# Keys, values and queries by Strassen's scheme: seven half-size products for eight in five of six column groups

## The chip, the cores and the metric

One core of one Trainium2 chip runs the whole program. The metric is the device time of one execution in microseconds (us); lower is better. The core has five engines that run side by side and meet at semaphores: TensorE (PE, matmuls; PEld is its weight load), VectorE (DVE), ScalarE (ACT), GpSimd (POOL) and SyncE (SP, which here only issues DMAs). PE writes PSUM, which has eight banks of 512 f32 columns on 128 partitions; POOL can't read PSUM.

## The reference, cut to what matters

One inference step of a two-layer decoder trunk, for 1024 prompt tokens and 64 sample tokens (1088 rows), D = 1024, all in float32. Layer 0 is a recurrent layer, layer 1 is differential attention over keys and values projected from the normed residual. The change touches only this:

```python
k, v = jnp.split(rms_norm(h, g) @ w_kv, [W_DIFF], axis=-1)            # W_DIFF = 768
k = rope(rms_norm(k.reshape(bsz, t, DIFF_HEADS, 2, DIFF_HD), k_g), pos)   # heads of 64
q, mem_q, gate = jnp.split(xn @ w_in, [W_DIFF, W_DIFF + W_MEM], axis=-1)
q = rope(rms_norm(q.reshape(bsz, t, DIFF_HEADS, 2, DIFF_HD), q_g), pos)
```

So three products of a 1088 x 1024 matrix with a 1024 x 768 one; keys and queries are then normed by head and rotated, and keys and values are also outputs.

## The kernel before

The program is a row of stages, each closed by a barrier. The stage that is changed, `keys_values_queries` (tiles named kvq_...), stands between `last_sums_and_norm` (which leaves the normed residual transposed in `xT`, and already computes tiles 2 and 3 of the first group, AHEAD) and the memory attention of layer 1.

The 2304 output columns are cut into six groups of W = 384 columns: k0, v0, k1, v1, q0, q1 (`GRP`). The rows are cut into NTILE = 9 tiles: NT = 8 prompt tiles of 128 rows and one sample tile of 64. For group i PE runs, for each prompt tile, KC = 8 matmuls (one for each 128 rows of the contraction) of `xT` 128 x 128 against 384 columns of `w[i % 2]` into one of the PSUM banks 0 to 5 (L2165), and for the sample tile 16 small ones (L2162). A float32 matmul shows in the trace as two instructions, so a tile of 384 columns is 16. The buffer `w` is double: SP loads the weights of group i when the products of group i - 2 are done (L2097), and POOL multiplies them by the norm's gain (`gained_weights`, L2111) before PE may start on them.

ACT takes each tile out of PSUM: for v a copy to `V`; for k and q a square (L2223) and a copy to `raw` (L2224). DVE reduces the squares by head (L2260). When the nine tiles of a group are there, ACT turns the sums into inverse roots (L2227, L2228, each with a table load), and DVE norms and rotates the whole group in eight operations over all nine tiles (L2263 to L2274) into `rot`, while PE is in the next group. Then PE transposes `rot` tile by tile through banks 6 and 7 (`turn`, L2147), and ACT copies to `KT` or `QT` (`turn_out`, L2188). POOL also issues the stores of k from `rot` (L2127) and of v from `V` (L2122).

At the end of the stage come the memory queries and gates (class `MemoryQueries`, `mem`): six jobs m on PE of 1088 columns each, with their weights loaded by SP (`mem.load`) and multiplied by the gain on POOL (L1422), and the weights of the first gates (`gates.load_ahead`, `gates.pool_ahead`, L1592). PE's order behind the last group is: turns of q0, jobs 0 and 1, turns of q1, jobs 2 to 5. `mem.act` of jobs 0 and 1 squares what `mem.dve` copied out of PSUM (L1472), and it stands ahead of the turns of q1 on ACT; on DVE `mem.dve` stands behind the norm of q1.

An instruction wrapped in `link(...)` is waited for by its own engine before the next is issued.

## Time and profile before

| | |
|---|---|
| median of 3 runs | 2091.23 us (2090.42 to 2688.17) |
| the profiled execution, its own time | 2090.91 us |
| its span in the profile | 2088.9 us |
| PE busy | 1937.7 us, 93% of the span |
| DVE, ACT, POOL busy | 42%, 30%, 17% |
| the stage's products, first to last group | 1152.4 to 1417.7 us |

A profile is one execution. Each instruction has a start and a duration; "idle before" is how long its engine stood still in front of it, with the instruction (engine, tile, line) that released it. PE's clock has two levels here, 2.4 GHz (shown as 1.00) and 1.2 GHz (0.50).

### The profile page before, as it was taken

Reading aid. Unit: us, or ns where it says so; the run is one execution under the profiler, and the core shown is the slowest. Engines: PE = TensorE matmul, PEld = TensorE weight load, DVE = VectorE, ACT = ScalarE, POOL = GpSimd, SP = SyncE. Lnnn points to the kernel's source line nnn. Section 1 sums busy time; section 2 is a strip of 40 time slices with the busy share of each in tenths; the row PEclk is TensorE's granted clock in tenths of the full one; section 3 lists DMA queues with packets and bytes.
Section 4 is the critical chain, followed back from the end, with each engine's and each line's share of the span. In section 5 each row is a group of like instructions: output and inputs, shape, how many; then the busy total and the mean of one; then the engine's idle time right before and its main releaser. Section 6 shows DMA issues by size and latency. Waiting matters only on the chain. (4 is left out here: it accounts for less than half of the span.)

```text
span 2088.9 us, 43622 instructions
## 1 busy us (share of the span) xinstructions
PE 1937.7 (93%) x19054; PEld 1251.2 (60%) x19054; DVE 882.9 (42%) x1785; ACT 616.7 (30%) x1447; POOL 346.6 (17%) x295
## 2 busy tenths in 40 slices
PE   6999989999999899997998999998999899799997
PEld 3576575675756757654444555555556566566664
DVE  4354372552734536323324324054123688733232
ACT  6322222222222222122214212222233466611111
POOL 0100030120300303020001130321000466311010
PEclk9999999999999999999999999999999999899998
DMA  8010010100100101008002120300110100566662
GB/s 285 18 36 13 11 34 26 32 20 21 34 22 17 39 21 33 23 17 314 1 31 86 61 95 31 134 11 10 41 61 21 61 1 1 203 223 223 216 221 76
DMA packets 53936, 147.61 MB, mean 71 GB/s; under 512 B 11587, under 2 KB 21123, under 8 KB 52468
## 3 DMA queue, kind: packets, MB, share of 16 engines
q1 hardware_dynamic: 43764, 103.97, 14.6%
q0 software_dynamic: 9984, 40.87, 5.6%
q8 instruction: 150, 2.46, 0.5%
q14 instruction: 38, 0.31, 0.0%
HBM read 123.58 MB, written 21.24 MB: 69 GB/s over the span
## 5 line engine op out<-in xcount | busy, mean ns | idle before, releaser
L772 PE MATMUL psum<-xT,rw_w 128*128 128x384 f32 (+1 forms) x1152 | 403.3, 489 | 0.0
L772 PEld LDWEIGHTS psum<-xT,rw_w 128*128 128x128 f32 x1152 | 206.4, 191 | 115.9 <-issue 11.3
L2165 PE MATMUL psum<-kvq_w,xT 128*128 128x384 f32 x384 | 124.6, 487 | 0.0
L1362 DVE SCALAR_TENSOR_TENSOR rwkv_xs<-psum,rwkv_pc,rwkv_xsc 128x64 f32<-128x64 f32 x90 | 25.5, 284 | 230.0 <-PE psum L1027 230.0
L2165 PE MATMUL psum<-spare,xT 128*128 128x384 f32 x352 | 114.3, 487 | 1.5 <-PEq L169 1.5
L740 POOL DMA_DIRECT2D out<-rwkv_s x6 | 5.8, 975 | 649.3 <-ACT rwkv_out_p L1172 649.3
L2165 PEld LDWEIGHTS psum<-kvq_w,xT 128*128 128x128 f32 x384 | 72.7, 190 | 50.9 <-issue 0.8
L1618 PE MATMUL psum<-xT,gate_w 128*128 128x384 f32 (+1 forms) x288 | 93.9, 474 | 1.8 <-PEq L169 1.8
L2165 PEld LDWEIGHTS psum<-spare,xT 128*128 128x128 f32 x352 | 66.6, 190 | 47.7 <-issue 1.7
L1150 ACT COPY rwkv_r_sb<-psum 128x64 f32<-128x64 f32 x96 | 20.3, 212 | 252.3 <-PE psum L1005 249.9
L1542 PE MATMUL psum<-xT,y_r 128*128 128x512 f32 (+1 forms) x180 | 87.0, 616 | 8.1 <-DMA y_r<-gated 8.1
L2260 DVE TENSOR_REDUCE kvq_ss<-kvq_sq 128x6 f32<-128x384 f32 (+1 forms) x36 | 19.9, 552 | 173.2 <-ACT kvq_sq L2223 163.5
L2649 PE MATMUL psum<-V,yT 128*128 128x512 f32 x192 | 92.7, 604 | 0.0
L2851 ACT COPY xT<-psum 128x384 f32<-128x384 f32 x64 | 30.6, 477 | 167.7 <-PE psum L2760 167.6
L919 PE MATMUL psum<-rwkv_dd,rwkv_am 64*64 64x64 f32 x1968 | 67.8, 219 | 11.5 <-issue 11.4
L2885 DVE COPY xT<-psum 128x384 f32<-128x384 f32 x64 | 35.6, 556 | 94.5 <-PE psum L2760 94.5
L2349 PE MATMUL psum<-KT,QT 64*128 64x512 f32 (+3 forms) x336 | 61.4, 480 | 14.2 <-ACT xT L2400 12.8
L1618 PEld LDWEIGHTS psum<-xT,gate_w 128*128 128x128 f32 x288 | 52.5, 190 | 33.5 <-issue 6.6
L2760 PEld LDWEIGHTS psum<-base,kp 128*128 128x128 f32 x384 | 48.0, 149 | 33.2 <-issue 26.6
L919 PEld LDWEIGHTS psum<-rwkv_dd,rwkv_am 64*64 64x64 f32 x1968 | 62.8, 135 | 7.3 <-issue 7.3
L801 PE MATMUL psum<-xT,rw_w 128*128 128x384 f32 (+1 forms) x192 | 66.7, 484 | 0.0
L1356 DVE COPY rwkv_sa_sb<-psum 128x64 f32<-128x64 f32 x96 | 21.5, 224 | 104.1 <-PE psum L1020 103.3
(454 smaller groups left out, 3872.8 us busy)
## 6 DMA issues: line engine op xcount, KB each, us to landing
kp<-in_cache_k SPq DMA_DIRECT2D x64, 384.0 KB, 4.1
xT<-in_cache_v POOLq DMA_DIRECT2D x48, 384.0 KB, 4.2
rw_w<-in_w_in SPq DMA_DIRECT2D x28, 512.0 KB, 3.7
gate_w<-in_cache_v POOLq DMA_DIRECT2D x16, 384.0 KB, 5.5
front_w<-in_mem_w_kv SPq DMA_DIRECT2D x2, 2048.0 KB, 14.7
x_rows<-in_x_p SPq DMA_DIRECT2D x8, 512.0 KB, 13.6
h<-in_x_p SPq DMA_DIRECT2D x8, 512.0 KB, 12.8
residual<-h POOLq DMA_DIRECT2D x8, 512.0 KB, 2.9
```

The source lines that it names most:

```text
L772: mm = pe.matmul(out, w[:, load % 2, k, :], xT[:, k, a:b], start=(k == 0), stop=(k == KC - 1))
L801: mm = pe.matmul(out, w[:, load % 2, k, :], xT[:, k, a:b], start=(k == 0), stop=(k == KC - 1))
L919: mm = pe.matmul(level_bank(g)[d, u, :], am[d, n, 0, :], dd[d, n, :], start=True, stop=True)
L1362: ins = nc.vector.scalar_tensor_tensor(out=xn, in0=bank[:, 3, 0:HS], scalar=pc[:, p % 2, n:n + 1], in1=xsc[:, :], op0=ALU.mult, op1=ALU.add)
L1542: mm = pe.matmul(self.bank[0:r, 5 + 2 * (u % 2), :], self.ys[k][:, n * P:n * P + r], self.w[:, k, half * 512:(half + 1) * 512], start=(k = ...
L1618: mm = pe.matmul(out, self.w[:, c % 2, k, :], self.xT[:, k, a:b], start=(k == 0), stop=(k == KC - 1))
L2165: mm = pe.matmul(bank[0:r, j % 6, 0:W], xT[:, k, n * P:n * P + r], w[i % 2][:, k, :], start=(k == 0), stop=(k == KC - 1))
L2349: mm = pe.matmul(both(m, is_big)[:, c, a:b], QT[d, h, i * P:(i + 1) * P], KT[d, h, a:b], start=True, stop=True)
L2649: mm = pe.matmul(self.out(u), self.ys[k][:, n * P:(n + 1) * P], self.w[k][:, half * 512:(half + 1) * 512], start=(k == 0), stop=(k == KC - 1))
L2760: mm = pe.transpose(bank[:, 4 + half, i * P:(i + 1) * P], kp[:, g % KR, (H3 * half + i) * P:(H3 * half + i + 1) * P], ident[:, :])
L2851: nc.scalar.copy(kT[:, g % TR, 0, :], bank[:, 4, 0:H3 * P]).then_inc(act_out, 1)
L2885: nc.vector.tensor_copy(kT[:, g % TR, 1, :], bank[:, 5, 0:H3 * P]).then_inc(dve_out, 1)
```

## The change

In groups 1 to 5 the eight prompt tiles are taken as four row pairs: rows m and m + 4 (the upper and lower half of the rows). With the contraction and the 384 columns halved as well, each row pair is a 2 x 2 product of blocks, which Strassen's scheme (in Winograd's form) does in seven block products for eight. A block product is KH = 4 matmuls of 128 x 128 against 192 columns into a bank of its own. Group 0 and the sample tile of each group stay as they were; the sample tile now comes first in its group.

- The left factors' sums `S` (four of 2048 columns a partition) are made once, on DVE, between the reductions of group 0.
- The right factors' sums are made on POOL for each group behind the gain: three of 768 columns (the last in two pieces), and a fourth (`first_factor`) in place in `w`, once the sample tile is through.
- The seven parts of a row pair are put together on DVE by seven additions of 192 columns, each with one operand in PSUM; ACT copies only the first part. `free_ring` lets PE reuse one of six banks when the part six places earlier has been read for the last time.
- ACT takes the squares of a normed group from SBUF, when all additions of the row pair are done.
- DVE norms and rotates not a group at a time but a row pair at a time (and the sample tile alone, behind row pair 1), in the order norm of group i - 1, then the additions of group i, with the reductions of group i ahead of both.
- PE's transposes of k0 and k1 are interleaved with the products of groups 2 and 4; those of q0 and q1 stay at the end. `norm_begins` now waits for the transposes of the group before ahead of all eight operations, not behind the first two.
- The memory queries' weights are loaded when the products of group 4 are done, the first gates' weights when those of group 5 are (their buffers hold factors and sums until then).

The diff, cut to its core:

```diff
+        PARTS = ("11x11", "s2xt2", "s3xt3", "12x21", "22xt4", "s1xt1", "s4x22")
+        READ_BY = (0, 1, 2, 3, 4, 6, 7)
+        def part_bank(x, j):
+            return bank[:, ring(1 + x // ROWS, 1 + len(PARTS) * (x % ROWS) + j), 0:HW]
...
         def _(sp):
...
+            wait_products(sp, LAST - 1)
+            mem.load(sp, 0)
             mem.load(sp, 1)
             mem.load(sp, 2)
+            wait_products(sp, LAST)
             gates.load_ahead(sp)
-            sp.wait_ge(mm_done, NTILE * 5)
-            mem.load(sp, 0)
             mem.load(sp, 3)
...
             def gained_weights(i):
...
-                nc.gpsimd.tensor_tensor(w[i % 2], w[i % 2], bcast(g.unsqueeze(2), [P, KC, W]), ALU.mult).then_inc(gained, 1)
+                link(nc.gpsimd.tensor_tensor(w[i % 2], w[i % 2], bcast(g.unsqueeze(2), [P, KC, W]), ALU.mult))
+                pool.sem_inc(gained, 1)
+                if i >= 2:
+                    wait_products(pool, i - 2)
+                t3, t2, t4 = FACTORS[i % 2]
+                link(nc.gpsimd.tensor_tensor(t3[0][1], quarter(i, 1, 1), quarter(i, 0, 1), ALU.subtract))
+                link(nc.gpsimd.tensor_tensor(t2[0][1], t3[0][1], quarter(i, 0, 0), ALU.add))
+                for k0, t in t4:
+                    n = t.shape[1]
+                    ins = nc.gpsimd.tensor_tensor(t, quarter(i, 1, 0)[:, k0:k0 + n, :], t2[0][1][:, k0:k0 + n, :], ALU.subtract)
+                    ins.then_inc(factors_ready, 1)
+            def first_factor(i):
+                pool.wait_ge(small_mm, i)
+                nc.gpsimd.tensor_tensor(quarter(i, 0, 1), quarter(i, 0, 1), quarter(i, 0, 0), ALU.subtract).then_inc(first_ready, 1)
...
             for i, (kind, half) in enumerate(GRP):
+                if i >= 1:
+                    first_factor(i)
+                if i < LAST:
                     gained_weights(i + 1)
...
+                for j, (left, right) in enumerate(((X(0, 0), B(0, 0)), (S_(1), T_(1)), (S_(2), T_(0)), (X(0, 1), B(1, 0)),
+                                                   (X(1, 1), T_(2)), (S_(0), B(0, 1)), (S_(3), B(1, 1)))):
+                    free_ring(pe, i, 1 + len(PARTS) * m + j)
+                    if m == 0 and j == 1:
+                        pe.wait_ge(factors_ready, 2 * i)
+                        pe.wait_ge(sums_ready, 1)
+                    if m == 0 and j == 5:
+                        pe.wait_ge(first_ready, i)
+                    for k in range(KH):
+                        mm = pe.matmul(part_bank(x, j), left(k), right(k), start=(k == 0), stop=(k == KH - 1))
+                    mm.then_inc(part_mm, 1)
+                    if i in TURNS_IN and j in (2, 5):
+                        turn_tile(TURNS_IN[i], 2 * m + j // 5)
...
+            def sums(i, m):
+                def add(out, one, j):
+                    nc.vector.tensor_tensor(out, one, part_bank(x, j), ALU.add).then_inc(added, 1)
+                add(c12, c11, 1)
+                add(c22, c12, 2)
+                add(c11, c11, 3)
+                add(c21, c22, 4)
+                add(c22, c22, 5)
+                add(c12, c12, 5)
+                add(c12, c12, 6)
...
+            for i in range(1, len(GRP)):
+                for m in range(ROWS):
+                    if own is not None:
+                        for t in ((0,) if m == 0 else (2 * m - 1, 2 * m)):
+                            reduced(own, t)
+                    if g is not None:
+                        if m == 0:
+                            norm_begins(g)
+                        tile_norm(g, order[m], 2)
+                        if m == 1:
+                            tile_norm(g, NT, 1)
+                    sums(i, m)
```

`tile_norm(g, n, count)` is the old group's eight operations on `count` tiles: two of 384 x count columns and six of 192 x count, the last of each dependent pair linked. `own` is the normed group's number of group i itself (None for v), `g` that of group i - 1.

## Rows read from the trace of the kernel before

**Rows 1.** The page's busy line, and its row for the changed products

```profile
PE 1937.7 (93%) x19054; PEld 1251.2 (60%) x19054; DVE 882.9 (42%) x1785; ACT 616.7 (30%) x1447; POOL 346.6 (17%) x295
L2165 PE MATMUL psum<-kvq_w,xT 128*128 128x384 f32 x384 | 124.6, 487 | 0.0
```

**Rows 2.** Timeline (start, length), PE: group 1, its turns, into group 2

```profile
1186.25 41.55 PE L2165 MATMUL psum<-kvq_w,xT 128*128 128x384 f32 x128
1227.73 2.82 PE L2162 MATMUL psum<-kvq_w,xT 128*64 128x192 f32 x32
1230.48 0.88 PE L2147 MATMUL psum<-base,kvq_rot 128*128 128x128 f32 x6
1231.97 0.93 PE L2147 MATMUL psum<-base,kvq_rot 128*128 128x128 f32 x6 [0.62 <-ACT KT L2188]
...
1235.65 41.55 PE L2165 MATMUL psum<-spare,xT 128*128 128x384 f32 x128
```

**Rows 3.** Timeline, PE: behind the last products, turns of q0 and q1

```profile
1417.73 0.88 PE L2147 MATMUL psum<-base,kvq_rot 128*128 128x128 f32 x6
1422.94 4.07 PE L2147 MATMUL psum<-base,kvq_rot 128*128 128x128 f32 x18 [4.34 <-ACT QT L2188]
...
1427.56 14.89 PE L1438 MATMUL psum<-xT,spare 128*128 128x292 f32 x48
1442.29 14.79 PE L1438 MATMUL psum<-xT,y_m 128*128 128x292 f32 x48
1456.92 0.82 PE L2147 MATMUL psum<-base,kvq_rot 128*128 128x128 f32 x6
1459.97 4.46 PE L2147 MATMUL psum<-base,kvq_rot 128*128 128x128 f32 x21 [2.24 <-ACT QT L2188]
1464.36 14.89 PE L1438 MATMUL psum<-xT,y_m 128*128 128x292 f32 x48
```

**Rows 4.** Timeline, PE, layer 1's attention: matmuls of 128 columns

```profile
1702.43 1.85 PE L2360 MATMUL psum<-V,xT 128*128 128x128 f32 x14
1708.49 1.50 PE L2360 MATMUL psum<-V,xT 128*128 128x128 f32 x12
```

**Rows 5.** Timeline, DVE: the norm of k0 (no POOL work beside it)

```profile
1190.94 3.76 DVE L2263 TENSOR_TENSOR kvq_raw<-kvq_raw,kvq_ss 128x3456 f32<-128x3456 f32 x1 [3.33 <-ACT kvq_ss L2228]
1194.73 3.76 DVE L2264 TENSOR_TENSOR kvq_raw<-kvq_raw,rows 128x3456 f32<-128x3456 f32 x1
1198.53 1.96 DVE L2269 TENSOR_TENSOR kvq_rot<-kvq_raw,late 128x1728 f32<-128x1728 f32 x1
1208.49 1.96 DVE L2274 TENSOR_TENSOR kvq_rot<-kvq_rot,kvq_raw 128x1728 f32<-128x1728 f32 x1
```

**Rows 6.** Timeline, DVE and POOL: the norm of q0, with POOL at work

```profile
1377.21 1.90 POOL L1422 TENSOR_TENSOR spare<-spare,vecs 128x1024 f32<-128x1024 f32 x1 [40.55 <-DMA spare<-in_b_in]
1379.06 10.79 POOL L1422 TENSOR_TENSOR y_m<-y_m,vecs 128x1024 f32<-128x1024 f32 x2
1378.19 4.53 DVE L2263 TENSOR_TENSOR kvq_raw<-kvq_raw,kvq_ss 128x3456 f32<-128x3456 f32 x1 [3.33 <-ACT kvq_ss L2228]
1382.75 5.34 DVE L2264 TENSOR_TENSOR kvq_raw<-kvq_raw,rows 128x3456 f32<-128x3456 f32 x1
1388.13 3.54 DVE L2269 TENSOR_TENSOR kvq_rot<-kvq_raw,late 128x1728 f32<-128x1728 f32 x1
```

**Rows 7.** Groups by line and form: short operations of DVE and POOL

```profile
L1560 DVE TENSOR_TENSOR h<-h,psum 128x512 f32<-128x512 f32 x16 | 11.0, 687 | 43.8 <-PE psum L1542 43.8
L2448 DVE TENSOR_TENSOR psum<-psum,late 128x256 f32<-128x256 f32 x48 | 20.4, 424 | 4.6 <-PE psum L2349 4.6
L2260 DVE TENSOR_REDUCE kvq_ss<-kvq_sq 128x6 f32<-128x384 f32 x32 | 17.7, 553 | 163.7 <-ACT kvq_sq L2223 163.5
L2431 POOL TENSOR_TENSOR xT<-xT 128x512 f32<-128x512 f32 x12 | 15.2, 1268 | 1.0
L2431 POOL TENSOR_TENSOR xT<-xT 128x128 f32<-128x128 f32 x12 | 5.5, 456 | 1.0
L740 POOL DMA_DIRECT2D out<-rwkv_s x6 | 5.8, 975 | 649.3 <-ACT rwkv_out_p L1172 649.3
```

**Rows 8.** Timeline, SP and POOL around group 2's start: weights, gain, stores

```profile
1230.59 0.33 SPq L2097 DMA_DIRECT2D kvq_w<-in_kv_w  x1
1210.76 4.83 POOL L2127 DMA_DIRECT2D out<-kvq_rot  x9 [46.39 <-DVE kvq_rot L2274]
1237.78 5.31 POOL L2111 TENSOR_TENSOR kvq_w<-kvq_w,vecs 128x3072 f32<-128x3072 f32 x1 [5.58 <-DMA kvq_w<-in_kv_w]
```

**Rows 9.** Stretches: engines' busy time and PE's clock, around PE's idle time

```profile
1418.60:1422.90 4.30, 0.00 (x1) 0.00 (x0) 0.97 (x2) 4.21 (x8) 0.00 (x0) 1.00 0.00 0
1422.90:1426.30 3.40, 3.36 (x14) 2.56 (x15) 3.37 (x2) 2.18 (x5) 0.00 (x0) 0.52 0.00 0
1426.40:1428.00 1.60, 1.38 (x10) 0.96 (x9) 1.60 (x1) 1.21 (x5) 0.00 (x0) 0.98 0.00 0
```

## What the change will do to the time, told before it was timed

> **What bounds the kernel now.** Read the busy line first: PE is busy for 93% of the span, and the changed products are its second largest group [rows 1]. Then read the timeline of one group: 128 instructions of 384 columns follow each other in 41.55 us, and the sample tile, the turns and the next group stand right behind [rows 2]. In five groups PE waits for nothing but ACT's copies between turns, some 1 us a group. So the stage lasts as long as PE's instructions do: groups 1 to 5 with the turns of k0 and k1 take 1186.25 to 1417.73, 231.5 us. DVE has the norm beside it, 1190.94 to 1210.45, 19.5 us of a group's 44 [rows 5], and otherwise reductions. PE has slack nowhere, DVE and POOL have much. The change takes work from PE and gives it to these two; the question is whether the slack lies where the new order needs it.
>
> **PE's own part.** One instruction of 384 columns costs (41.55 - 0.49) / 127 = 323.3 ns [rows 1, 2]; at 2.4 GHz and two clocks a column, which this row fits, 384 columns are 320, so 3.3 ns lie on top. For 192 columns that gives 163.3 ns. No row shows 192 columns against a full 128 x 128 load; the nearest, 128 columns, come at (1.85 - 0.28) / 13 = 121 ns and (1.50 - 0.28) / 11 = 111 ns [rows 4], 4 to 14 ns above their 106.7. So the bounds are 163 and 175 ns; I take 163.3, since the excess falls where matmul and load have the same length. A row pair was 32 x 323.3 ns = 10.35 us and becomes 7 x 4 x 2 = 56 x 163.3 ns = 9.15 us. Over 20 row pairs that is -24.0 us (-10.9 at 175 ns). The sample tile keeps its 2.75 us. The turns of k0 and k1 took 5.17 us each [rows 2]; their 27 instructions alone, at 0.12 us, are 3.2, and between products ACT's copies no longer hold them up: -3.9 us. A group would last 2.75 + 4 x 9.15 = 39.35 us, and 42.6 with turns. If nothing else mattered, PE would gain 28 us.
>
> **DVE's part.** Operations of 3456 and 1728 columns take 3.76 and 1.96 us and follow after 0.03 us [rows 5]: 1.04 ns a column and 0.16 us fixed. So 768, 384 and 192 columns cost 0.99, 0.59 and 0.39 us start to start. An operand in PSUM changes little: 512 columns take 687 ns, 256 take 424 [rows 7], on the same line. The norm of two tiles is 2 x 0.99 + 6 x 0.59 = 5.5 us, that of the sample tile 2 x 0.59 + 6 x 0.39 = 3.5, a group's 25.6 us instead of 19.5. Seven additions are 2.7 us a row pair, 10.9 a group. Two reductions are 1.2 [rows 7]. The left sums, 4 x 2.3 us in group 0, lie between reductions 5 us apart and cost nothing.
>
> **How long PE can wait for it.** The additions of a row pair free five of the six banks. Part 8 (the first of row pair 1) needs the bank read by the first addition of row pair 0; the same holds for each next pair. DVE does a norm between the additions of two pairs, so after them PE has seven parts, 9.15 us, of cover. Row pair 1 has 5.5 + 3.5 = 9.0 us of norm ahead of its additions: just covered. In groups 2 and 4 DVE has only 2.7 + 1.2 us a row pair, so these take 42.6 us each.
>
> **Where POOL comes in.** The norm of q0 had POOL at work beside it [rows 6]. DVE's first operation took 4.53 us instead of 3.76, the second 5.34, the third 3.54 instead of 1.96; POOL's two took 10.79 us where one alone takes 1.90. The ends fit turns: POOL's first runs to 1379.1 and DVE then takes its 3.7; POOL's second waits until 1382.7 and takes 1.9; DVE's second waits for that and ends at 1388.1. In all DVE lost 3.9 us to two POOL operations of 1.9. So each microsecond that POOL works during a norm is one that DVE stands, and an operation holds the other for its whole length. The Trainium skill, "SBUF — State Buffer" (Summary: rules for kernel authors), says the same: a VectorE operation with two SBUF inputs and a GpSimd one that reads SBUF block each other entirely. By that rule, the trace agrees, additions with one PSUM input are not blocked; no row here shows it.
>
> What does POOL do in a norm's time? The gain of the next group takes 5.31 us and starts 7.2 us after SP's load is issued, which is at the group's start [rows 8]. In the kernel before it happened to lie behind the stores, beside no norm. Now it comes first. Behind it stand the new factors. POOL's operations on two full inputs cost 456 ns for 128 columns and 1268 for 512 [rows 7], so 2.1 ns a column and 0.19 us: 1.8 us for 768 columns, 1.4 and 0.6 for the split one. That is 5.3 + 5.6 = 10.9 us of POOL.
>
> **Group 1, from its start T.** The inverse roots are ready at T + 4.7 [rows 5, 2]. DVE does three operations to T + 7.3; the gain holds it to 12.6; the other five (3.0 us) alternate with the four factors (5.6) to T + 21.3. The first addition ends at 21.8. PE had done row pair 0 at 2.75 + 9.15 = 11.9, so it stands 9.9 us. Behind 4.3 us of idle time its clock was 0.52 for 3.4 us [rows 9]; that costs 1.7 us of work. Row pair 1 ends at 32.7; the next addition at 33.5 (24.0 + 9.0 of norm + 0.5): 0.8 us more. Two row pairs follow: the group lasts 51.8 us instead of 39.35. Group 3 starts its norm 0.9 us later, since two squares and reductions come first: 52.6 us.
>
> **Group 5** has three memory gains on POOL (1.90 each), of which about 3.4 us fall into the norm, and reductions of its own with a wait for ACT's squares, 1.8 us a row pair. First addition: norm from T + 6.8, 5.5 + 3.4, 0.4: 16.1, a stall of 4.2. Second: 18.5 + 1.8 + 9.0 + 0.4 = 29.7; PE was through at 26.9 with its slow clock: 2.8. Again 1.7 of slow clock, which leaves no third stall. Row pairs 2 and 3 take it to 49.7.
>
> **The tail.** Before, turns of q0 resumed 4.7 us behind the last product, once ACT had its roots done, and ended 9.8 behind it [rows 3]. Now the last additions, two squares from SBUF and two reductions come first: +2.7 us. The norm of q1 waits for all turns of q0, starts at +12.5, takes 25.6 us, and POOL's last gain and two gate gains (5.7 us) fall into it: +43.8. Jobs 0 and 1 on PE end at 12.5 + 29.4 = +41.9; then ACT must square what DVE copies only behind the norm before it may take the turns. Copy, two squares, nine turns end at +52.5; before it was 1464.36 - 1417.73 = 46.6. So +5.9 us.
>
> **Moved steps that cost nothing.** POOL's queue in group 2: stores of k0 may start when its norm ends, 2.1 us before the group's last product; 18 stores at 0.54 us [rows 8] end 7.6 us into group 2, and `first_factor` at 9.4; PE needs it behind the sample tile, five parts and a turn, at 9.8. That is covered by 0.4 us only. The memory weights wait for group 4, and are needed a group later.
>
> **The sum.** 51.8 + 42.6 + 52.6 + 42.6 + 49.7 = 239.3 us against 231.5: +7.8. With the tail +13.7. The profiled execution took 2090.9 us (span 2088.9), which becomes 2104.6; the median of the runs is 0.3 above: 2105 us.
>
> **Rivals.**
> 1. *DVE and POOL do not hold each other up in operations this short.* Then group 1's additions come at T + 12.3, row pair 1's norm just misses (0.6 us): 40 us each for groups 1 and 3, 46.3 for group 5 by its reductions alone, tail +2.7. Sum 211.5 - 231.5 + 2.7 = -17.3: 2074 us, faster than before. For it: the lock is seen on long operations only. Against it: three DVE operations of two lengths all fit the turns. It decides if less than 3 us of the 10.9 are lost. Chance 0.16.
> 2. *PE alone sets the time.* Additions and norms are cheaper than summed and hidden: -28 us, 2063. Chance 0.05.
> 3. *POOL's queue is late in groups 2 and 4.* A store of another kind takes 975 ns [rows 7]; 18 of these instead of 0.54 us put `first_factor` 7.5 us late, twice: 2120 us. Chance 0.12.
> 4. *The load no longer hides behind a matmul.* The Trainium skill, "TensorE: Matmul & The Clock Gate" (What overlaps and what doesn't), lets a load overlap a running matmul only in other row groups. The trace disagrees: the load's row shows 190 ns, yet matmuls follow at 323 and 111 ns. As a mechanism of this kernel: load and matmul of 192 columns in series would come at about 107 + 160 = 267 ns, the first from the spacing at 128 columns [rows 4], +104 ns x 1120 = +116 us: 2207. Chance 0.02.
> 5. *The forecast*, DVE late by its norm, its additions and POOL's hold in groups 1, 3 and 5: 0.62, its own range 2094 to 2117. The remaining 0.03 is something not seen.
>
> **Range and chances.** From rival 1 to rival 3: 2070 to 2122. Within 2% of 2091.2 is 2049 to 2133; 2% is about what a measurement of this kernel can tell from no change. PE's whole gain is 1.3%, so over 2% faster is all but excluded: 0.01. Over 2% slower needs rival 4, or rival 3 on top of the forecast with long stores: 0.06. Within: 0.93.
>
> **What would show it.** In the profile after: 192-column products 163 ns apart; groups 2 and 4 of 42 to 43 us, 1, 3 and 5 of 50 to 53, with PE idle 8 to 11 us for the first additions' sake at row pair 1 of groups 1 and 3; DVE operations of row pair 0's norm stretched to 6 us once and to 2 us some four times; PE's clock at 0.5 behind it. The forecast is wrong if the gain on POOL and the norm of row pair 0 overlap without either becoming longer, if PE idles for POOL's `first_ready`, or if an addition costs much more than 0.36 us.

## The result and the profile after

The changed kernel took 2095.15 us (median; 2089.06 to 2097.87) against 2090.04 us for the kernel before on the same chips: a ratio of 1.0021, with a 95% interval of 1.0011 to 1.0031. A second comparison gave 2096.03 against 2089.30 us, 1.0029 (1.0017 to 1.0041). So it became slower by some 5 to 7 us, 0.2 to 0.3%. 13.7 us were forecast. One run of the kernel before, at 2688 us, stands far outside the others and does not enter the ratio. The profiled execution took 2097.87 us, its span 2096.2 us.

The busy line of the page after: PE has 16 us less work than in [rows 1], DVE 94 and POOL 41 us more, and the span is 7 us longer.

```profile
PE 1921.7 (92%) x19534; PEld 1321.4 (63%) x19534; DVE 977.0 (47%) x2058; ACT 606.1 (29%) x1427; POOL 387.2 (18%) x320
```

The PE timeline after (start us, length us, engine, line, tiles, count, and in brackets the idle time before it and what ended it): group 1, where [rows 2] show one row of 41.55 us, then the starts of groups 2 to 5, and the waits in groups 3 and 5.

```profile
1186.30 2.77 PE L2246 MATMUL psum<-kvq_w,xT 128*64 128x192 f32 x32
1189.00 1.57 PE L2276 MATMUL psum<-kvq_w,xT 128*128 128x192 f32 x8
...
1206.53 2.93 PE L2276 MATMUL psum<-kvq_w,xT 128*128 128x192 f32 x8 [8.16 <-DVE V L2433]
...
1217.95 1.46 PE L2276 MATMUL psum<-kvq_w,xT 128*128 128x192 f32 x8
...
1236.24 2.82 PE L2246 MATMUL psum<-spare,xT 128*64 128x192 f32 x32
...
1278.56 2.82 PE L2246 MATMUL psum<-kvq_w,xT 128*64 128x192 f32 x32
...
1298.31 2.93 PE L2276 MATMUL psum<-kvq_w,xT 128*128 128x192 f32 x8 [7.64 <-DVE V L2433]
...
1328.21 2.82 PE L2246 MATMUL psum<-spare,xT 128*64 128x192 f32 x32
...
1370.53 2.82 PE L2246 MATMUL psum<-kvq_w,xT 128*64 128x192 f32 x32
...
1385.88 2.92 PE L2276 MATMUL psum<-kvq_w,xT 128*128 128x192 f32 x8 [3.23 <-DVE spare L2433]
```

Group 1 lasts 1236.24 - 1186.30 = 49.94 us. PE does row pair 0, waits 8.16 us for the first addition of V (L2433), and then runs slowly for a while: eight products take 2.93 us instead of 1.57. The same stands in groups 3 and 5; groups 2 and 4 have no such wait.

The DVE and POOL timelines after, for those 8.16 us:

```profile
1191.09 0.96 DVE L2466 TENSOR_TENSOR kvq_raw<-kvq_raw,kvq_ss 128x768 f32<-128x768 f32 x1 [3.34 <-ACT kvq_ss L2340]
1192.09 0.96 DVE L2467 TENSOR_TENSOR kvq_raw<-kvq_raw,rows 128x768 f32<-128x768 f32 x1
1193.08 0.56 DVE L2468 TENSOR_TENSOR kvq_rot<-kvq_raw,late 128x384 f32<-128x384 f32 x1
1193.55 5.67 DVE L2469 TENSOR_TENSOR kvq_rot<-kvq_raw,late 128x384 f32<-128x384 f32 x1
1199.26 2.04 DVE L2470 TENSOR_TENSOR kvq_raw<-kvq_raw,late 128x384 f32<-128x384 f32 x1
1201.22 2.15 DVE L2471 TENSOR_TENSOR kvq_raw<-kvq_raw,late 128x384 f32<-128x384 f32 x1
1203.41 1.64 DVE L2472 TENSOR_TENSOR kvq_rot<-kvq_rot,kvq_raw 128x384 f32<-128x384 f32 x1
1204.96 0.94 DVE L2473 TENSOR_TENSOR kvq_rot<-kvq_rot,kvq_raw 128x384 f32<-128x384 f32 x1
1206.12 2.19 DVE L2433 TENSOR_TENSOR V<-V,psum 128x192 f32<-128x192 f32 x7 [0.21 <-DVE kvq_rot L2473]
```
```profile
1193.34 5.47 POOL L2187 TENSOR_TENSOR spare<-spare,vecs 128x3072 f32<-128x3072 f32 x1 [2.37 <-DMA spare<-in_kv_w]
1198.98 1.90 POOL L2192 TENSOR_TENSOR y_m<-spare 128x768 f32<-128x768 f32 x1 [0.18 <-POOL spare L2187]
1200.96 2.00 POOL L2193 TENSOR_TENSOR y_m<-y_m,spare 128x768 f32<-128x768 f32 x1
1203.04 1.59 POOL L2196 TENSOR_TENSOR y_m<-spare,y_m 128x576 f32<-128x576 f32 x1
1204.59 0.90 POOL L2196 TENSOR_TENSOR spare<-spare,y_m 128x192 f32<-128x192 f32 x1
```

An operation of 384 columns takes 0.56 us alone. The one that meets POOL's gain takes 5.67, and the next four take 2.04, 2.15, 1.64 and 0.94 while POOL's four factors take 1.90, 2.00, 1.59 and 0.90: they take turns, the forecast's picture of group 1. The turns are cheaper than the forecast had them, though: each DVE operation ends 0.41 us behind the POOL operation before it (1203.37 behind 1202.96, say), where alone it takes 0.56.

The stretches of the PE clock after (stretch, length, busy time and count of PE, PEld, DVE, ACT, POOL, then PE clock, DMA share, GB/s): just behind the wait, and groups 1 to 5 whole.

```profile
1206.50:1209.90 3.40, 3.37 (x11) 3.38 (x12) 3.33 (x8) 0.32 (x1) 0.00 (x0) 0.50 0.00 0
1186.30:1416.50 230.20, 211.17 (x1338) 205.94 (x1334) 147.55 (x282) 39.60 (x92) 80.60 (x64) 0.94 0.18 64
```

A granted clock of 0.50 is the lower of the two levels, 1.2 GHz. Groups 1 to 5 last 230.2 us, of which PE stands still for 19: hardly less than the 231.5 us of before, when it was never kept waiting but for the turns. PE's gain has been turned into waiting.

The PE timeline after of the tail, to set beside [rows 3]:

```profile
1416.47 0.82 PE L2240 MATMUL psum<-base,kvq_rot 128*128 128x128 f32 x6
1422.64 4.12 PE L2240 MATMUL psum<-base,kvq_rot 128*128 128x128 f32 x18 [5.35 <-ACT QT L2318]
...
1460.84 5.00 PE L2240 MATMUL psum<-base,kvq_rot 128*128 128x128 f32 x21 [3.21 <-ACT QT L2318]
1465.76 15.52 PE L1438 MATMUL psum<-xT,y_m 128*128 128x292 f32 x48
```

From the first turn to the third job the tail takes 1465.76 - 1416.47 = 49.3 us (46.6 before; 52.5 forecast), and that job's first row then has the slow clock too: 15.52 us instead of 14.89.

### The profile page after: what moved, and what is told of

It is laid out like the page before. It is cut to its first block and busy times, and to the rows that moved or that the text cites. A ratio compares the mean times of both kernels' runs of the same rounds, so it can differ in the third digit from the quotient of the medians.

```text
span 2096.2 us, 44928 instructions
## 1 busy us (share of the span) xinstructions
PE 1921.7 (92%) x19534; PEld 1321.4 (63%) x19534; DVE 977.0 (47%) x2058; ACT 606.1 (29%) x1427; POOL 387.2 (18%) x320
## 5 line engine op out<-in xcount | busy, mean ns | idle before, releaser
L1362 DVE SCALAR_TENSOR_TENSOR rwkv_xs<-psum,rwkv_pc,rwkv_xsc 128x64 f32<-128x64 f32 x90 | 25.5, 284 | 230.2 <-PE psum L1027 230.2
L919 PE MATMUL psum<-rwkv_dd,rwkv_am 64*64 64x64 f32 x1968 | 67.9, 219 | 11.8 <-issue 11.4
L2994 PEld LDWEIGHTS psum<-base,kp 128*128 128x128 f32 x384 | 47.6, 148 | 34.5 <-issue 26.4
L2983 POOL DMA_DIRECT2D xT<-in_cache_v x48 | 25.8, 538 | 224.6 <-PE psum L3039 180.1
L2994 PE MATMUL psum<-base,kp 128*128 128x128 f32 x384 | 57.6, 289 | 7.1 <-ACT xT L3085 3.9
L1331 DVE TENSOR_TENSOR rwkv_mm<-psum,masks 128x256 f32<-128x256 f32 (+1 forms) x132 | 49.2, 396 | 31.3 <-PE psum L919 29.1
L2594 PE MATMUL psum<-V,xT 128*128 128x128 f32 x432 | 62.4, 289 | 1.3 <-ACT xT L2656 1.3
L1141 ACT COPY rwkv_dd<-psum 128x256 f32<-128x256 f32 (+1 forms) x108 | 37.2, 356 | 87.4 <-PE psum L934 68.3
```

Of the source, the lines that this page charges most:

```text
L919: mm = pe.matmul(level_bank(g)[d, u, :], am[d, n, 0, :], dd[d, n, :], start=True, stop=True)
L1141: nc.scalar.copy(dd[:, group(g), :], level_bank(g)).then_inc(d_ready, 1)
L1331: nc.vector.tensor_tensor(mm_[:, group(g), :], level_bank(g), bcast(const_view(const, f"pair{b}").unsqueeze(1), [P, n, CH]), ALU.mult).the ...
L2594: mm = pe.matmul(bank[:, 7, 0:P], wT[:, j * P:(j + 1) * P], V[:, j, h * P:(h + 1) * P], start=(j == 0), stop=(j == i))
L2994: mm = pe.transpose(bank[:, 4 + half, i * P:(i + 1) * P], kp[:, g % KR, (H3 * half + i) * P:(H3 * half + i + 1) * P], ident[:, :])
```

## The experiments

The theory under test, H: the changed kernel loses PE's gain because DVE is late, and DVE is late mainly because POOL's gain and factors fall into the norm of row pair 0 and the two hold each other. The rivals: DVE's own work is too long (the norm and the additions, whatever POOL does), or POOL's work is late for PE. The second is out by the profile after: in groups 1 to 5 PE waits 15.8 us for the additions of V and 3.2 us for those of group 5, and never for POOL. The kernels e1 to e7 are the changed kernel with one edit each, or edits on top of each other. The table gives, for each, the ratio to the kernel before with its interval, the median, and from its PE timeline the length of groups 1 to 5 and of the stage from group 1's start to the head sums' product (before: 292.7 to 292.9 us in four profiles), in us. Lengths are those of one profile each, but for the stage of the changed kernel, which has three.

| kernel | ratio (95%) | median | g1 | g2 | g3 | g4 | g5 | stage |
|---|---|---|---|---|---|---|---|---|
| changed | 1.0029 (1.0017-1.0041) | 2096.0 | 49.9 | 42.3 | 49.7 | 42.3 | 45.9 | 294.8-295.4 |
| e1 | 0.9931 (0.9916-0.9946) | 2075.7 | 39.9 | 42.3 | 39.9 | 42.3 | 45.9 | 275.0 |
| e2 | 1.0043 (1.0027-1.0058) | 2099.6 | 50.9 | 42.3 | 52.1 | 42.3 | 47.5 | 298.0 |
| e3 | 0.9968 (0.9955-0.9981) | 2084.7 | 45.0 | 42.3 | 46.2 | 42.3 | 47.4 | 286.1 |
| e4 | 0.9954 (0.9940-0.9967) | 2080.0 | 39.9 | 46.3 | 39.9 | 44.6 | 45.9 | 280.3 |
| e5 | 0.9926 (0.9910-0.9942) | 2075.4 | 39.9 | 42.3 | 39.9 | 42.3 | 47.6 | 274.9 |
| e6 | 0.9896 (0.9881-0.9912) | 2069.3 | 39.9 | 42.3 | 39.9 | 42.3 | 43.9 | 269.8 |
| e7 | 0.9877 (0.9861-0.9893) | 2065.5 | 39.3 | 42.3 | 39.4 | 42.3 | 39.3 | 265.0 |

Group 5 lasts 45.9 us in some of them and 47.4 to 47.6 in others, with the same instructions in e1 to e5. It always has a wait of 3.23 us at row pair 1. Where the clock falls behind that one (changed, e1, e4), the next wait, at row pair 2, is at most 1.6 us. In e2, e3 and e5 the clock stays full behind it, the next wait is 2.9 us, and the clock falls behind that. So 1.6 us of group 5 belong to where the clock fell and not to the edits.

**e1: without POOL's work for groups 2 and 4.**

```diff
                 pool.wait_ge(w_loaded[i % 2], 16 * ((i + 1) // 2))
+                if i in (2, 4):
+                    pool.sem_inc(gained, 1)
+                    pool.wait_ge(added, len(PARTS) * (ROWS * (i - 2) + 1))
+                    pool.sem_inc(factors_ready, 2)
+                    return
```

> Leaves out POOL's gain and factor sums for groups 2 and 4 (so their keys and queries are wrong); DVE's norms and additions stay as in the changed kernel. Theory H (hold: POOL's reads and DVE's two-input operations exclude each other, each microsecond of POOL costs DVE one): the norm of row pair 0 in groups 1 and 3 shrinks from about 15 us to 5.3, PE's waits of 8.2 and 7.6 us and the slow clock behind them vanish, groups 1 and 3 go from 49.9 and 49.7 to 39.5 to 41 us each: about 19 us less, ratio to before about 0.993. Rival D (DVE's own work is what makes PE wait, POOL only happens to run beside it): row pair 0's norm still ends late, groups 1 and 3 stay above 45 us, at most 8 us less.

The PE timeline of e1: row pair 1 of group 1, where the 8.16 us stood, and then row pair 2.

```profile
1202.98 1.46 PE L2281 MATMUL psum<-kvq_w,xT 128*128 128x192 f32 x8
...
1212.52 1.57 PE L2281 MATMUL psum<-kvq_w,xT 128*128 128x192 f32 x8 [0.28 <-DVE V L2438]
```

The DVE timeline of e1, the norm of row pair 0 with nothing on POOL, from its first operation to the first addition:

```profile
1195.86 0.96 DVE L2471 TENSOR_TENSOR kvq_raw<-kvq_raw,kvq_ss 128x768 f32<-128x768 f32 x1 [3.33 <-ACT kvq_ss L2345]
...
1200.44 0.55 DVE L2478 TENSOR_TENSOR kvq_rot<-kvq_rot,kvq_raw 128x384 f32<-128x384 f32 x1
1201.21 1.80 DVE L2438 TENSOR_TENSOR V<-V,psum 128x192 f32<-128x192 f32 x6 [0.21 <-DVE kvq_rot L2478]
```

The norm takes 5.1 us instead of 14.8. The wait of 8.16 us is gone; in its place PE waits 0.28 us one row pair later. The group lasts 39.85 us, 10.1 less. Of the 10.1, 7.9 are waits and the rest is the slow clock behind them. The whole kernel becomes 20 us faster than the changed one: two groups at some 10. DVE's own work is therefore not what holds PE in groups 1 and 3.

**e2: POOL's work held back until row pair 0 is added.** One line, in the same place:

```diff
+                if i in (2, 4):
+                    pool.wait_ge(added, len(PARTS) * (ROWS * (i - 2) + 1))
```

> Same work as the changed kernel, but POOL's gain and factor sums for groups 2 and 4 start only when row pair 0's additions in groups 1 and 3 are done. Theory H: the hold is moved, not removed. Row pair 0 passes without a wait; the norm of row pair 1 (8.4 us) takes about 20, its first addition comes at 32 us into the group, PE waits some 11 us there, and one full row pair fewer is left behind it: groups 1 and 3 of 51 to 54 us, together 3 to 7 us more than the changed kernel, ratio to before 1.003 to 1.006. Rival P (only the place right in front of the first additions hurts, since PE has just seven parts of cover there): groups 1 and 3 of 40 to 44 us, ratio about 0.994.

The PE, DVE and POOL timelines of e2:

```profile
1216.88 2.93 PE L2278 MATMUL psum<-kvq_w,xT 128*128 128x192 f32 x8 [9.84 <-DVE V L2435]
```
```profile
1199.30 5.95 DVE L2469 TENSOR_TENSOR kvq_raw<-kvq_raw,rows 128x768 f32<-128x768 f32 x1
```
```profile
1198.55 5.89 POOL L2189 TENSOR_TENSOR spare<-spare,vecs 128x3072 f32<-128x3072 f32 x1 [8.01 <-DVE V L2435]
```

Row pair 1 is now on time and row pair 2 waits 9.84 us: the same hold one norm later, behind a DVE operation of 768 columns that takes 5.95 us instead of 0.96. So it is not the moment of the weights' arrival that costs, but that POOL works beside a norm at all. The norms of row pair 1 and of the sample tile together take 17.9 us instead of 8.4.

**e3: the gain of groups 2 and 4 on ACT.** POOL keeps only the factors.

```diff
-                link(nc.gpsimd.tensor_tensor(w[i % 2], w[i % 2], bcast(g.unsqueeze(2), [P, KC, W]), ALU.mult))
-                pool.sem_inc(gained, 1)
+                if i in (2, 4):
+                    pool.wait_ge(gained, i)       # else as before
 ...
+            def act_gain(i):                      # ACT, behind the copy of row pair 0 of groups 1 and 3
+                for k in range(KC):
+                    ins = nc.scalar.activation(w[i % 2][:, k, :], w[i % 2][:, k, :], ACT.Copy, scale=g[:, k:k + 1])
```

> The gain of groups 2 and 4 goes from POOL to ACT as eight scaled copies of 384 columns (about 3.8 us); the factor sums stay on POOL behind it. Theory H: the norm of row pair 0 is no longer held and ends 10.1 us into the group; the factors, 6 us of POOL from about 11 us on, fall into the norm of row pair 1, whose first addition comes at about 25.5: PE waits 4 us there instead of 8 at row pair 0, group 46 us instead of 49.8. Together 7 us less than the changed kernel: ratio to before 0.998 to 1.000. Rival (ACT does not read beside DVE for free, or the copies delay ACT's part copies): groups stay at 49 to 50.

The ACT and PE timelines of e3:

```profile
1197.79 4.16 ACT L2344 ACTIVATE spare<-spare,vecs 128x384 f32<-128x384 f32 x8 [1.16 <-DMA spare<-in_kv_w]
```
```profile
1215.74 2.40 PE L2279 MATMUL psum<-kvq_w,xT 128*128 128x192 f32 x8 [3.70 <-DVE V L2445]
```

ACT reads and writes the same weights and does so in 4.16 us beside the norm. With only the factors left on POOL, the waits fall from 8.16 and 7.64 to 3.70 and 4.15 us. Group 1 is 5.0 and group 3 3.5 us shorter. So in group 1 the gain is half of what POOL costs, and in group 3 a third; the rest is the factors, which now stand beside the norm of row pair 1. That norm and the sample tile's take 11.8 us together where 8.4 are needed: DVE loses 3.4. The kernel gained more than was expected of it (ratio 0.9968, expected 0.998 to 1.000).

**e4: the factors on DVE as well,** behind the last norm that DVE does in groups 1 and 3. POOL then has only `first_factor` of each group and the stores.

```diff
+                        if m == ROWS - 1 and i in (1, 3):
+                            dve_factors(i + 1)    # the same subtract, add and two subtracts, on nc.vector
```

> As the one before, but the factor sums of groups 2 and 4 are made by DVE itself behind the norm of row pair 3 in groups 1 and 3 (768 columns at 0.99 us each, 3.1 us in all, instead of 6 us of holding by POOL). Theory H: nothing is held; DVE has 4.8 + 24 + 9 + 3 = 41 us of work in a group and keeps ahead at each row pair, so groups 1 and 3 last 39.5 to 40.5 us, 19 to 20 us less than the changed kernel: 2075, ratio to before 0.9925. Rival D (DVE's own work is the bound even without POOL): groups 1 and 3 of 44 us or more, ratio 0.997 or above.

Groups 1 and 3 reach 39.9 us, as meant. But groups 2 and 4 grow from 42.3 to 46.3 and 44.6, against the expectation. The PE and POOL timelines of e4 in group 2:

```profile
1235.32 2.13 PE L2282 MATMUL psum<-spare,QT 128*128 128x192 f32 x8 [2.03 <-POOL spare L2207]
```
```profile
1223.71 4.83 POOL L2212 DMA_DIRECT2D out<-kvq_rot  x9 [35.49 <-DVE spare L2498]
1228.53 4.81 POOL L2212 DMA_DIRECT2D out<-V  x9
1233.36 1.81 POOL L2207 TENSOR_TENSOR spare<-spare 128x768 f32<-128x768 f32 x1
```

This is the prediction's rival 3 at another size. `first_factor` of group 2 stands behind 18 stores. With groups 1 and 3 slow, these stores had begun before group 2 and the factor was in time (the prediction had 0.4 us to spare; in the profile after it ends 1.4 us before PE's sixth part); once group 1 ends 10 us earlier, they begin 0.3 us after group 2 does, and PE waits 2.0 us and then runs at the slow clock.

**e5: `first_factor` between the stores of k and those of v.**

```diff
-                if i >= 1:
+                if i in (1, 3, 5):
                     first_factor(i)
 ...
                         store(k_out, i - 1, n, rot[0:rows_of(n), n, :], k_stored)
+                    first_factor(i + 1)
```

> As e4_factors_dve, but on POOL the first factor of groups 2 and 4 stands ahead of the nine stores of v, behind the nine stores of k. In e4_factors_dve, where groups 1 and 3 last only 39.9 us, PE waited 2.0 us for that factor in each of groups 2 and 4 and ran on at the low clock (46.3 and 44.6 us instead of 42.3). Theory Q (the queue of 18 stores at 0.54 us is what is late): the factor ends 4.8 us earlier, the waits vanish, both groups last 42.3 us, 6 us less than e4_factors_dve: ratio to before 0.992 to 0.993. Rival: the factor is late for another reason (its own 1.8 us, or the wait for the sample tile), and nothing moves.

The POOL timeline of e5:

```profile
1225.54 4.84 POOL L2212 DMA_DIRECT2D out<-kvq_rot  x9 [35.48 <-DVE spare L2499]
1230.39 1.84 POOL L2207 TENSOR_TENSOR spare<-spare 128x768 f32<-128x768 f32 x1
```

The factor now starts 5.1 us into group 2 instead of 9.9 (1230.39 - 1225.27, against 1233.36 - 1223.44), the stores of v follow it, and groups 2 and 4 are back at 42.3 us. The kernel takes 2075 us, as little as e1, which leaves the gain and the factors out.

**e6: the gains of the memory weights moved away from the norms** of group 5 and of the tail. `mem.pool` now takes the first job and the last; before it did all four.

```diff
-            mem.pool(pool)
+            pool.wait_ge(ss_ready, NTILE * 4)
+            mem.pool(pool, 0, 3)
+            pool.wait_ge(rot_ready, CHUNKS * 4)
+            mem.pool(pool, 3, 4)
             gates.pool_ahead(pool)
```

> As e5_factor_first, and POOL's gains leave DVE's norms alone: those of the first three memory weights wait until the last reduction is done (DVE then waits for the turns of q0), the fourth and the gates' until the norm of q1 is done. Theory H: in group 5 the norm of row pair 0 is no longer held for 3.2 us, its first addition no longer late by 3.2 us; row pair 1's comes 1 to 2 us late at full clock; the group lasts 40.5 to 42 us instead of 45.9. Behind it the norm of q1 ends 4.8 us earlier, ahead of job 1's end, and the turns of q1 start 1 us earlier. Together 5 to 6 us less than e5_factor_first: ratio 0.989 to 0.9905. Rival D (reductions and additions bound group 5 whatever POOL does): group 5 stays above 44 us.

The POOL and PE timelines of e6:

```profile
1398.31 1.90 POOL L1422 TENSOR_TENSOR spare<-spare,vecs 128x1024 f32<-128x1024 f32 x1 [41.43 <-DVE spare L2430]
1400.17 3.75 POOL L1422 TENSOR_TENSOR y_m<-y_m,vecs 128x1024 f32<-128x1024 f32 x2
```
```profile
1376.02 2.46 PE L2286 MATMUL psum<-kvq_w,xT 128*128 128x192 f32 x8 [2.64 <-DVE spare L2452]
```

Two gains take 3.75 us, where in [rows 6] they took 10.79: nothing stands beside them. The wait of 3.23 us at row pair 1 is gone. Group 5 is 3.7 us shorter than in e5 and 2.1 shorter than where the clock fell earlier. The tail from group 5's end to the third job takes 46.8 us (1442.77 - 1396.01) instead of 48.1 in e5 and 49.3 in the changed kernel. Group 5 and tail together take 90.6 us, against 95.7 in e5 and 95.2 in the changed kernel. But 40.5 to 42 us were expected of group 5 and it lasts 43.9: PE still waits 2.64 us at row pair 2, and the clock falls behind that. No POOL operation stands beside the norms there, so this is DVE's own work, which in group 5 has reductions in front of each norm. The median is 2069.3 us, 1.0% below the kernel before: this version beats both.

**e7: PE alone, from the other side.** The norms of k0, k1 and q0 cut to one operation each, POOL's work as in the changed kernel.

```diff
+                if g < 3:
+                    nc.vector.tensor_tensor(out, x, bcast(rs.unsqueeze(3), [r, count, 6, HS]), ALU.mult).then_inc(rot_ready, 1)
+                    return
```

> The changed kernel with seven of the eight operations of each norm of k0, k1 and q0 left out (keys and queries are not rotated and lack their gain, so outputs are wrong); POOL's work, the additions and all of PE's work stay. Bounds what PE alone gives. Theory: PE waits for nothing in groups 1 to 5; these last 39.4, 42.3, 39.4, 42.3, 39.4 us = 202.8 instead of 230.2, 27 us less: ratio to before 0.989. Rival A (the additions with their PSUM operand and the six-bank ring hold PE up by themselves): groups 1, 3 and 5 stay above 42 us.

No group has a wait. Groups 1, 3 and 5 last 39.3 us: what the prediction's working gave for PE alone, 39.35. The whole, 2065.5 us, is close to its rival 2 (2063). The hold itself is still there: two norm operations of 768 columns that meet POOL's factors take 4.69 us together. But with one operation left of each norm DVE stays in time, and POOL's work costs PE nothing. This run leaves out DVE's own work as well, so it bounds what PE can gain and does not price the hold; that is what e1 does.

**The kernels before and changed, again.** Three more profiles of the one and two of the other, to see what outside the stage repeats.

> The kernel before once more, for a second profile. In all profiles with changed products the stretch from the first gates' product to the first scores takes 133.1 us or more, in the one profile of the kernel before 131.4, with the same instructions; there the clock fell to half for 3.4 us behind an idle time of 1.99 us, and in the kernel before it did not. Theory C (the moment decides whether that idle time lets the clock fall, and the moment shifts with what ran before): this profile may show either 131.4 or 133.1. Rival S (something of the changed stage carries over, such as a late transfer): 131.4 again.

> A third profile of the kernel before. Theory C: at least one of the two stretches behind the stage (131.4 and 293.2 us in both profiles so far) now takes 1.5 us or more longer, as in the profiles of the changed kernels. Rival S: 131.4 and 293.2 again.

> A fourth profile of the kernel before, with the same two theories and numbers as b2_before_again.

> The changed kernel again, timed beside the kernel before. Its stage, from the start of group 1 to job 2, took 1.35 us more than before, but the median of its runs lies 5 us higher and its span 7.3 us; outside the stage no instruction differs. Theory C (where the clock falls to half outside the stage changes from execution to execution and belongs to neither kernel): the stage repeats within 0.5 us (279 to 280 us against 278.1), the stretches outside it vary by 1 to 5 us between executions of one kernel, and the ratio is 1.000 to 1.003. Rival S (the changed stage makes what follows slower every time): the stretches behind it, from the first gates' product to the first scores and from the last values to the end, again take 133 and 295 us or more.

> A third profile of the changed kernel, for the spread of the stretches outside the stage, with the same two theories and numbers as a2_after_again.

One stretch of unchanged code differs each time. From the first gates' product to the first scores it takes 131.4 us in all four profiles of the kernel before and 133.0 to 133.1 us in all three of the changed one (133.0 to 134.7 in the seven experiments). The PE timeline of it, first of the kernel before and then of the changed one:

```profile
1542.52 0.66 PE L1734 MATMUL psum<-base,mem_both 128*128 128x128 f32 x4 [1.99 <-DVE mem_both L1873]
1543.01 2.32 PE L1618 MATMUL psum<-xT,gate_w 128*128 128x320 f32 x8
```
```profile
1544.61 0.66 PE L1734 MATMUL psum<-base,mem_both 128*128 128x128 f32 x4 [1.99 <-DVE mem_both L1873]
1545.10 4.00 PE L1618 MATMUL psum<-xT,gate_w 128*128 128x320 f32 x8
```

The stretches of the clock, in the same order:

```profile
1543.00:1545.00 2.00, 2.00 (x10) 1.45 (x9) 0.00 (x0) 0.59 (x1) 0.00 (x0) 1.00 0.03 8
```
```profile
1547.00:1549.00 2.00, 2.00 (x5) 1.11 (x5) 0.00 (x0) 0.00 (x0) 0.00 (x0) 0.50 0.00 0
```

The same instructions after the same 1.99 us of idle time run at full clock in the one kernel and at half in the other, 1.7 us dearer. That holds for all profiles of the two kernels, and for six of the seven experiments. In e3 the clock stays full there (2.32 us again) and had fallen some 40 us earlier, at the first gates' product, behind an idle time of some 1.9 us that all kernels have there. In e4, e6 and e7 it falls at both places: these are the three with 134.7 us. The end of the run is less steady: from the last values' product to the end of the span it takes 293.1, 293.3, 296.2 and 293.1 us before, and 296.5, 296.0 and 296.2 after, 2.3 more on average. At the very end the low clock lasts some 10 us in three profiles of the kernel before, and some 14 in the fourth (the one with 296.2) and in the changed kernel. With 2.4 us in the stage (295.1 against 292.7 on average) this makes 2.4 + 1.7 + 2.3 = 6.4 us, between the 5.1 and 6.7 that the two comparisons of medians gave. Two theories were told ahead: that the place where the clock falls changes from execution to execution (C), or that something of the changed stage carries over each time (S). For the stretch of 131.4 us the profiles speak for S. For the end neither is settled, where one profile of the kernel before looks like the changed one. By what the stage carries over stays open: the records show the clock and what stood just before it, and these are alike.

## Why the prediction was right in kind and wrong in size

In us, the changed kernel's profile against the prediction's working:

| step | forecast | measured |
|---|---|---|
| group 1 | 51.8 | 49.9 |
| groups 2, 4 | 42.6 each | 42.3 each |
| group 3 | 52.6 | 49.7 |
| group 5 | 49.7 | 45.9 |
| groups 1 to 5, against before | +7.8 | -1.3 |
| tail, against before | +5.9 | +2.7 |
| behind it, against before | 0 | +3.7 to +5.3 by the two medians, of which 0.6 in the third job |

**PE's own part held.** Eight products of 192 columns take 1.46 us, (1.46 - 0.33) / 7 = 162 ns apart, against 163.3 forecast, also with the full load that no row of before showed; rival 4 is out. The two groups without a stall last 42.3 us, and e7 gives 39.3 for the others. PE alone is worth 231.5 - (39.3 + 42.3 + 39.4 + 42.3 + 39.3) = 28.9 us; 28 were forecast.

**The mechanism held.** The hold, its place, the two groups it strikes and the clock behind it are as told; e1 and e2 show it from two sides, by taking POOL's work away and by moving it, and rival 1 (no hold in short operations) is out with the operation of 5.67 us. The Trainium skill, "SBUF — State Buffer" (Summary: rules for kernel authors), has VectorE and GpSimd block each other where VectorE reads two inputs from SBUF. That an addition with one operand in PSUM escapes had no row before. Here it does escape. In group 2 the additions of row pair 0 (L2433) stand beside POOL's gain and take no longer than elsewhere, nor does the gain. The POOL and DVE timelines of the changed kernel:

```profile
1245.74 5.31 POOL L2187 TENSOR_TENSOR kvq_w<-kvq_w,vecs 128x3072 f32<-128x3072 f32 x1 [1.17 <-DMA kvq_w<-in_kv_w]
```
```profile
1246.20 0.35 DVE L2433 TENSOR_TENSOR kvq_raw<-kvq_raw,psum 128x192 f32<-128x192 f32 x1 [1.02 <-PE psum L2276]
1249.13 0.35 DVE L2433 TENSOR_TENSOR kvq_raw<-kvq_raw,psum 128x192 f32<-128x192 f32 x1 [1.08 <-PE psum L2276]
```

**What failed is the size of the hold and of DVE's own operations, all a little too long.** In group 1 the first addition ends at T + 20.2 us instead of 21.8, and PE waits 8.16 us instead of 9.9. Two terms of the prediction make this up.

- *"Each microsecond that POOL works during a norm is one that DVE stands."* In "the other five (3.0 us) alternate with the four factors (5.6)" the two are added up, 8.6 us; it took 7.1 (1198.81 to 1205.90). The whole norm lost 14.8 - 5.1 = 9.7 us to POOL work put at 10.9: 1.2 us less. The rows of before had this already: in [rows 6] the third operation lost 3.54 - 1.96 = 1.58 us to a POOL operation of 1.9. An operation that is held loses 0.2 to 0.3 us less than the POOL operation lasts, and with five POOL operations in a row that counts.
- *"Operations follow after 0.03 us"* was read between operations of which each needs the one before. Where the next does not need it, it starts before the other's end: in e1, 0.47 us after a start, though each lasts 0.56; seven additions of 0.35 us take 2.19, not 2.7. So the norm of two tiles takes 5.1 us, not 5.5, that of the sample tile 3.1, not 3.5, and the two reductions of a row pair with their wait some 1.5, not 1.8.

Groups 3 and 5 also start their norm earlier than forecast, at T + 4.6 instead of 5.6 and at T + 5.8 instead of 6.8. So in group 3 one DVE operation more passes ahead of the gain: 7.64 us against the 10.7 that its forecast of 52.6 holds. In group 5 the norm itself takes the 8.9 us forecast, and the wait is 3.23 against 4.2.

**The second stalls were over-forecast.** The prediction had 0.8 us in group 1, as much in group 3, and 2.8 in group 5, where row pair 1's norms of 9.0 us met 9.15 us of cover and in group 5 the reductions came on top. The norms take 8.4 us (1208.22 to 1216.59), and the slow clock gives PE more to do in the meantime. In groups 1 and 3 no second stall came. In group 5 none shows in the profile above, but the two later profiles of the same kernel have one of 1.5 us there (in a2_after_again at 1396.81). The group lasts 45.9 us with it and without it: what the clock takes less, the wait takes more. The clock itself cost more than the 1.7 us forecast: row pair 1 of group 1 takes 1217.95 - 1206.53 = 11.4 us instead of 9.1, so 2.3 us. The sum for group 1 closes: 39.35 + 8.16 + 2.3 = 49.8 us, measured 49.94.

**The tail** was mis-sized in the same way. Turns of q0 resume 1422.64 - 1416.47 = 6.2 us behind the first of them, 1.0 us more than before [rows 3] where 2.7 were forecast, and the norm of q1 ends 40.1 us behind it instead of 43.8. That the gains beside that norm cost time is right: with them away from it the tail went from 48.1 (e5) to 46.8 us (e6).

**Cost outside the stage was forecast as nothing.** Here some 4 us of the 5 to 7 measured ones arise in code that the change did not touch: 1.7 us by the clock at one place, shown above, and 2.3 at the end, where the low clock lasts longer. In the stage itself the change is worth +2.4 us.

So the forecast of 13.7 us had 11.3 us too much in the stage and lacked some 4 us outside it. The largest parts of the 11.3 are the first waits of groups 1, 3 and 5 (24.8 us forecast, 19.0 measured), the second ones (4.4 forecast, none or 1.5 measured) and the tail (3.2 too much); against them stands the slow clock, which cost 0.6 us more than forecast in each of groups 1 and 3 and another 0.6 in the third job. The median lies inside the range of 2070 to 2122 us, but it is chance that it is no further from 2105: the two errors go opposite ways.

One rival was also summed on the wrong base: rival 4 adds its 116 us to the kernel before, though its 104 ns are over the 163 ns of PE's own part. On that part's 2063 us it gives 2179, not 2207. Nothing else hangs on it.

## What to carry to other kernels

Before work is moved to POOL, list what DVE reads at that time: a POOL operation beside a DVE one with both operands in SBUF costs DVE nearly its whole length. Here 11 us of "free" POOL work took 9.7 us from a norm, and with the slow clock behind it ate 10 us of PE's time in each of two groups. The cure is a matter of who and when: here the gain of 5.3 us done by ACT in 4.2 us, 5.6 us of factors by DVE itself in 3.0, one operation moved up in POOL's queue, and the memory gains placed where DVE does no norm: together 27 us from the change as first built (2096 to 2069). When the first limit goes, read the queues again, since an order that had 1.4 us of slack turned into a wait of 2 us (e4). And sum short DVE operations by their measured spacing, linked and unlinked apart, not by length plus a gap.

## What the runs showed of the hardware that was not expected

- A DVE operation held by POOL pays by operations, not by its own length: operations of 384 columns took 5.67 us beside a gain of 5.47, and 2.04, 2.15, 1.64 and 0.94 us beside factors of 1.90, 2.00, 1.59 and 0.90. DVE doing the factors itself (3.0 us in e4) is no dearer for DVE than standing beside POOL doing them (3.4 us lost in e3).
- DVE operations that do not need each other overlap: 0.31 us from start to start for 192 columns, which last 0.35, and 0.47 for 384, which last 0.56.
- Idle time on PE of the same length is not always followed by the low clock. Behind the 1.98 to 1.99 us in the rows above it fell in nine of ten profiles of changed kernels and in none of four of the kernel before; behind a wait of 3.23 us in group 5 it fell in five profiles and stayed full in three (e2, e3, e5). It costs 1.7 us at the first place, and 2.3 us behind the waits of groups 1 and 3.
